# One diffusion-backbone layer on one core: 28 table slabs split and stored ahead of their stage, and one meeting of the engines where there were three

## The reference, cut to what matters

```python
# the merge behind the two mixers
(sigmoid(ga) * (attn @ w_up_a) + sigmoid(gb) * (ret @ w_up_b)) @ w_o
# PEER, in blocks of 128 tokens
s1, s2 = scores of the two query halves against 128 keys each, for 8 heads
16 best of each side, 16 best of their sums -> e (128 experts a token), g = softmax
a = gelu(x @ u_tab[e]);   out = (g * a) @ v_tab[e]
```

## Time and profile before

| | |
|---|---|
| Median of three runs | 2513.26 us |
| The profiled execution: its own time, its span | 2514.28 us, 2512.5 us |
| Busy share of the span | PE 91%, DVE 74%, ACT 48%, POOL 15% |
| Mean granted TensorE clock | 0.953 |
| Merge stage | 623.5 to 900 us |
| Table stage: LEAD, tiles, TAIL | 906 to 1097, 1097 to 1708.6, 1708.6 to 1801 us |
| Second table, residual, norm | 1809.5 us to the end |

### The profile page before, as it was taken

One profiled execution on the slowest core, in us unless ns is written; L12 is line 12 of the kernel. 1 busy time (PEld: TensorE's weight loads), 2 busy tenths in 40 slices (PEclk: granted clock), 3 DMA queues, 4 the chain that ended last, 5 costly groups with the idle time before them and its releaser, 6 DMA issues. The chain is left out here.

```text
span 2512.5 us, 34243 instructions
## 1 busy us (share of the span) xinstructions
PE 2290.0 (91%) x12048; PEld 1257.8 (50%) x12048; DVE 1857.6 (74%) x4157; ACT 1202.7 (48%) x1694; POOL 371.0 (15%) x267
## 2 busy tenths in 40 slices
PE   6799997985898979889899898999799999999997
PEld 3477664442665754435545455465344444444443
DVE  2555416455655357889989999885689999999999
ACT  1433433235444225555455454565645555555553
POOL 0000000000000000122222122232122222222220
PEclk9899998997998989999999899999899999999999
DMA  9421221000522144564676766889788778777881
GB/s 385 188 77 59 96 76 45 17 17 18 217 71 89 59 185 160 190 222 165 248 249 225 255 212 239 295 292 391 258 327 299 294 296 298 293 295 296 304 301 67
DMA packets 163392, 506.98 MB, mean 202 GB/s; under 512 B 14368, under 2 KB 47936, under 8 KB 155584
## 3 DMA queue, kind: packets, MB, share of 16 engines
q1 hardware_dynamic: 95440, 296.13, 33.0%
q0 software_dynamic: 36864, 134.23, 14.7%
q10 hardware_dynamic: 30960, 75.07, 7.8%
HBM read 421.93 MB, written 83.44 MB: 201 GB/s over the span
## 5 line engine op out<-in xcount | busy, mean ns | idle before, releaser
L210 ACT ACTIVATE lin_hi<-lin_raw,lin_wsc 128x1024 f16<-128x1024 f32 x196 | 224.3, 1146 | 414.5 <-DVE lin_wsc L123 326.3
L1747 POOL DMA_INDIRECT row<-u_rows_dram,picked x128 | 185.3, 1448 | 1505.8 <-DVE picked L2022 929.3
L231 PE MATMUL u_ps<-h_hi,lin_hi 128*128 128x512 f16 x1024 | 398.8, 389 | 7.5 <-PEq L64 7.5
L231 PE MATMUL u_ps<-h_lo,lin_hi 128*128 128x512 f16 x1024 | 397.6, 388 | 0.0
L231 PE MATMUL u_ps<-h_hi,lin_lo 128*128 128x512 f16 x1024 | 397.1, 388 | 0.0
L216 DVE SCALAR_TENSOR_TENSOR lin_lo<-lin_raw,lin_wsc,lin_hi 128x1024 f16<-128x1024 f32 x196 | 250.9, 1282 | 179.0 <-ACT lin_hi L210 178.9
L1683 POOL DMA_INDIRECT row<-v_dram,picked x128 | 178.4, 1394 | 490.8 <-DVE acc L2259 449.6
L175 ACT ACTIVATE lin_junk<-lin_raw 128x1024 bf16<-128x1024 f32 x196 | 204.5, 1043 | 62.9 <-DMA lin_raw<-w_all_dram 62.6
L2370 PE MATMUL y_ps<-region 128*128 128x512 f16 x512 | 194.9, 381 | 8.3 <-PEq L64 8.3
L2372 PE MATMUL y_ps<-region 128*128 128x512 f16 x512 | 194.8, 380 | 0.0
L2371 PE MATMUL y_ps<-region 128*128 128x512 f16 x512 | 194.8, 380 | 0.0
(11 more groups left out here) (378 smaller groups left out, 4124.1 us busy)
## 6 DMA issues: line engine op xcount, KB each, us to landing
lin_raw<-w_all_dram SPq DMA_DIRECT2D x196, 512.0 KB
act_scratch<-activated ACTq DMA_DIRECT2D x128, 256.0 KB
wgt_scratch<-region ACTq DMA_DIRECT2D x64, 512.0 KB
region<-v_dram SPq DMA_DIRECT2D x15, 2048.0 KB
oh_buf<-v_dram SPq DMA_DIRECT2D x15, 2048.0 KB
proj<-w_mod_dram SPq DMA_DIRECT2D x16, 1536.0 KB, 11.9
region<-wgt_scratch SPq DMA_DIRECT2D x16, 1024.0 KB, 9.7
region<-act_scratch SPq DMA_DIRECT2D x16, 1024.0 KB
```

What stands on the lines that cost most here:

```text
L210: nc.scalar.activation(self.hi[b][:], self.raw[b][:], ACT.Copy, scale=self.wsc[:, b:b + 1]).then_inc(self.sem("head", b), 1)
L231: last = nc.tensor.matmul(self.ps[b % 2][:, half, 0:ts.stop - ts.start], w_[:, kc, :], x_[:, kc, ts], start=(j == 0 and kc == 0), stop=(j ...
L1747: nc.gpsimd.indirect_dma_start(out=row[j % NG][:], out_offset=None, in_=a["u_rows"], in_offset=bass.IndirectOffsetOnAxis(ap=rows0[:, j:j + ...
```

## The change

Three things are done.

1. **28 slabs are split early.** They are those with b = 2 and 3 of the first 14 quads of the token tiles (quads `QA` to `QE` - 1: tiles 0 and 1 and the first 16 slabs of tile 2). Their loads, squares, heads and rests are made beside merge slabs 1 to 28, their scales four wide in the same instructions as those of the merge maps, and GpSimd's queue stores both halves (256 KB each) to a scratch array in device memory. In the tiles SP loads the two halves (2 x 256 KB) straight into `hi` and `lo`, where it loaded the raw slab (512 KB); ACT and DVE do nothing for these slabs but the gelu. The powers of two are kept in a small tile.
2. **`clear` becomes `retire` at three changes** (projection to attention, attention to merge, first to second table): only the block's own end is a meeting; GpSimd clears the dead semaphores inside the next block. The change from merge to first table keeps all three meetings.
3. **The last batch of a tile** is multiplied and evicted behind the next tile's first slab, and the tile loops of PE and SP are written out (they were hardware loops).

Core of the diff:

```diff
+            def load_pre(self, sp, q, b):
+                sp.wait_ge(self.sem("product", b), q)
+                for n, half in enumerate((self.hi[b], self.lo[b])):
+                    sp.dma_start(half[:, :, :].rearrange("p k m -> p (k m)"), pre_d[2 * (q - QA) + b - 2, n]
+                                 ).then_inc(s(f"pre_ld{b}"), 16)
...
             def product(self, pe, q, b, staged=None):
-                pe.wait_ge(self.sem("split", b), q + 1)
+                if self.pre(q, b):
+                    pe.wait_ge(s(f"pre_ld{b}"), 32 * (q - QA) + 32)
+                else:
+                    pe.wait_ge(self.sem("split", b), self.turn(q, b) + 1)
...
+                to = (q + (b + n) // 4, (b + n) % 4)
+                return to if b + n < 4 * left + 4 and not self.pre(*to) else None
...
                 @block.sync   # merge stage
+                    def load_pre_raw(sl):
+                        if (p := pre_slab(sl)) is not None:
+                            if p >= 4:
+                                sp.wait_ge(s("pre_split"), p - 3)
+                            sp.dma_start(pre_raw[p % 4][:], a["w_all"][4 * (QA + p // 2) + 2 + p % 2]).then_inc(...)
...
+                @block.gpsimd
+                def _(pool):
+                    for p in range(NPRE):
+                        pool.wait_ge(s("pre_split"), p + 1)
+                        for n, half in enumerate((pre_hi, pre_lo)):
+                            pool.dma_start(pre_d[p, n], half[p % 2][:]).then_inc(s(f"pre_st{p % 2}"), 16)
...
                 @block.scalar   # merge stage
+                    def pre_square(sl): ...          # waits for the load; ACT Square, as L175
+                    def pre_head(sl):
+                        if (p := pre_slab(sl)) is not None:
+                            act.wait_ge(lin.sem("scaled", p % 4 // 2), Q_UP + 2 + p // 4)
+                            if p >= 2:
+                                act.wait_ge(s(f"pre_st{p % 2}"), 32 * (p // 2))
+                            nc.scalar.activation(pre_hi[p % 2][:], pre_raw[p % 4][:], ACT.Copy, scale=...)
...
                         lin.act_slab(act, q, b, left)
+                        pre_head(sl + 3)
+                        pre_square(sl + 5)
...
                 @block.vector   # merge stage
+                    def pre_rest(sl): ...            # waits for pre_head; as L216, and a copy of one column
...
                         lin.dve_before(dve, q, b, left, inverse=sl + 1 not in (WO, WQ, LAST))
                         lin.dve_after(dve, q, b, left)
+                        pre_rest(sl + 3)             # ahead of the slab's eviction
...
                 def tile(t):    # table stage, PE
                     for m in range(PLAIN):
                         lin.pe_slab(pe, *at(t, m))
+                        if t and m == 0:
+                            gates(t - 1, NBATCH - 1)
...
-                    gates(t, NBATCH - 1)
-                run(pe, 0, NTD, tile)
+                for t in range(NTD):
+                    tile(t)
...
-        s.clear("vp_")
+        s.retire("vp_")
```

More of the change, by code:

```diff
@@ L153, in sem, with pre, turn, col @@
                 return s(f"{self.tag}_{what}{b}")
+            @staticmethod
+            def pre(q, b):
+                return b >= 2 and isinstance(q, int) and QA <= q < QE
+            @staticmethod
+            def turn(q, b):
+                if b < 2 or not isinstance(q, int) or q <= QA:
+                    return q
+                return QA if q < QE else q - (QE - QA)
+            @staticmethod
+            def col(b):
+                return slice(4 * (b // 2) + b % 2, 4 * (b // 2) + b % 2 + 1)
+            @staticmethod
+            def pre_col(p):
+                return slice(4 * (p % 4 // 2) + 2 + p % 2, 4 * (p % 4 // 2) + 3 + p % 2)
+            @staticmethod
+            def width(q):
+                return 4 if isinstance(q, int) and Q_UP < q < Q_U else 2
             @staticmethod
@@ new lines, in square @@
+            def square(self, act, q, b):
+                n = self.turn(q, b)
+                act.wait_ge(self.sem("loaded", b), 16 * n + 16)
+                act.wait_ge(self.sem("total", b // 2), n)
+                act.wait_ge(self.sem("square", (b + 3) % 4), n + 1 if b else self.turn(q, 3))
+                if b == 0 and self.pre(q - 1 if isinstance(q, int) else q, 3):
+                    act.wait_ge(self.sem("square", 1), q)
+                if b == 2:
+                    act.wait_ge(self.sem("square", 1), q + 1)
+                nc.scalar.activation(self.junk[:], self.raw[b][:], ACT.Square, accum_out=self.ssq[:, self.col(b)]
@@ L176, in square @@
                                      ).then_inc(self.sem("square", b), 1)
             def total(self, pe, q, g):
[L179 to L182, removed]
+                n, w = self.turn(q, 2 * g), self.width(q)
+                pe.wait_ge(self.sem("square", 2 * g), n + 1)
@@ L183, in total @@
+                pe.wait_ge(self.sem("square", 2 * g + 1), n + 1)
+                pe.wait_ge(self.sem("scaled", 1 - g), q + 1 if g else self.turn(q, 2))
+                if g == 0 and isinstance(q, int) and self.pre(q - 1, 2):
+                    pe.wait_ge(self.sem("scaled", 0), q)
+                if w == 4:
+                    pe.wait_ge(s("pre_sq"), 4 * (q - Q_UP - 1) + 2 * g + 2)
+                nc.tensor.matmul(self.total_ps[g][:, 0:w], ones[:], self.ssq[:, 4 * g:4 * g + w],
                                  start=True, stop=True).then_inc(self.sem("total", g), 1)
@@ L250, in wait_out, with ahead @@
                 eng.wait_ge(self.sem("product", b), q + 1)
-                eng.wait_ge(self.sem("inverse", b), self.inverses(q + 1))
+                if not self.pre(q, b):
+                    eng.wait_ge(self.sem("inverse", b), self.inverses(self.turn(q, b) + 1))
             def out(self, b):
                 return self.ps[b % 2][:, 0:2, 0:NH2]
-            @staticmethod
-            def ahead(q, b, n, left):
-                return (q + (b + n) // 4, (b + n) % 4) if b + n < 4 * left + 4 else None
+            def ahead(self, q, b, n, left):
+                to = (q + (b + n) // 4, (b + n) % 4)
+                return to if b + n < 4 * left + 4 and not self.pre(*to) else None
             def act_slab(self, act, q, b, left=2):
@@ L1688, in build @@
             NBATCH = P // OB
-            PLAIN, LEAD = 4, 32
             PIECES = 8
```

139 lines of the change are left out of this document (99 added, 40 removed).

## The result

The kernel after takes 2472.12 us (median, 2465.45 to 2473.3), beside 2513.94 us for the kernel before on the same chip: a ratio of 0.9828 (95% interval 0.9814 to 0.9842), 42 us less where 32 were forecast. The prediction of 2481 us was 9 us too high; the range 2467 to 2500 holds the result.

What follows compares the result with a forecast made beforehand. DVE was taken to bound the tiles, with PE nearly equal after the change, and PE the merge stage. Tiles -40, merge +15.2 and meetings -7.4 gave -32.2 us, so 2481 us against the 2513.26 median; range 2467 to 2500.

Steps and rivals of the forecast that it cites:

- a sum of 45.6 us: Tiles: DVE work and waits removed for 28 slabs, 12.2 + 16.7 + 16.7 us; 40 us taken as the gain.
- The last batch: Tile ends: PE's wait of up to 5.4 us goes, but its gain is inside the 40 us, not beside it.
- The merge stage, +15.2: Merge stage: added early-split work costs 15.2 us in sum, between 8 below and 30 above.
- UP, 8.1 us a slab and 9 in all: UP: early head and rest delay evictions, 8.1 us a slab where PE needs 6.6; 9 us over slabs 2 to 7.
- Start, 2.7: Merge start: the pair's total also needs two early slabs, 1 MB more in the load queue; 2.7 us.
- WO, 3.5 in a late eviction: WO: early head and rest make the eviction 0.7 us late, 0.3 at even b; 3.5 us over slabs 9 to 15.
- WQ and the stores, 0: WQ: added work hidden below PE's 6.6 us a slab; stores, estimated at 10 us at most, hidden too; 0.
- Meetings, -7.4: Three stage changes: second and third meetings dropped, with all of SP's waits there paid back; 7.4 us less.
- Clock in UP: Rival: merge stage pays twice as much, PE's clock falling in UP with its stops; 2494 us, chance 0.15.
- Half the gain: Rival: tiles gain only 25 us, PE and DVE holding each other up or halves arriving late; 2496 us, chance 0.12.
- The stores: Rival: in the merge stage the early head waits for the store of two slabs before; 2539 us at 16 us, chance 0.05.
- Hidden better, 2467: Rival: merge costs only 8 us and the tiles gain DVE's full 45.6 us; 2467 us, chance 0.08.

Runs made afterwards that it cites:

- run 4: Changed kernel with its merge-side work kept, but the tiles load and split every slab themselves as before: 2519.6 us, ratio 1.0016.
- run 5: Changed kernel with idle work on DVE in place of the 28 early slabs' rests and scales, 40 us in all: 2513.58 us, ratio 0.9991.
- run 7: Changed kernel with only 14 idle rests put back on DVE, 16.7 us: 2485.49 us, ratio 0.9872.
- run 6: Changed kernel with idle work on ACT, 28 copies and 28 squares, 61 us in all: 2470.27 us, ratio 0.9819.
- run 2: Kernel before with only the last batch moved behind the next tile's first slab and PE's and SP's tile loops written out: 2512.94 us, ratio 0.9995.
- run 3: Changed kernel with each tile's last batch back at the tile's end: 2474.55 us, ratio 0.9831.
- run 8: Changed kernel without the token tiles' 56 loads of halves and PE's wait for them, output part left out: 2472.45 us, ratio 0.9826.
- the seven and the three traces named above: Seven traces with the changed kernel's merge code, merge stage 295.3 to 299.6 us; three with the merge code before, 281.6 to 282.7 us.
- Run 11: As run 10, with loads of slabs 4 and 5 and the first two early slabs ahead of the gates' loads: 2463.67 us, ratio 0.9784.
- run 10: As run 9, with 32 slabs split early instead of 28: 2462.02 us, ratio 0.9789.
- run 9: Changed kernel with the early rest behind the slab's evictions in UP and WO instead of ahead of them: 2469.44 us, ratio 0.9819.
- Run 12: As Run 11, with early rest behind the next slab's scales, early square ahead of early head, x and keys loaded later: 2460.69 us, ratio 0.9781.
- run 1: Kernel before with one meeting instead of three at the three stage changes, nothing else: 2507.61 us, ratio 0.9971.

## Why the prediction was right, and where it was not

**The tiles.** The forecast took 40 us from a sum of 45.6 (14 rests, 10 pairs with their scales and a rest, 4 places of 3.05 us), because "PE and DVE are nearly equal, each waits for the other at times". Measured: 44.8 us from tile 0 to tile 3's picks, and 47 by the ratio of run 4, with its 5 us either way. Another 1.6 us are gone from the last six slabs of LEAD, but not by DVE's relief: in run 5, with DVE's work put back, these six still take 32.8 us (34.5 before, 32.9 in the changed kernel). Slab 30 of LEAD takes 6.1 us before, 5.2 after and 6.4 in run 4, where the early slabs are squared and totalled in the tiles again; the forecast had counted nothing for those totals. **The step that failed is the loss of 5.6 us put on that sum.** PE's busy time was taken as given, 448.8 of 449.9, but 16.4 us of it went with the waits: 432.3 us at a granted clock of 0.99, from 448.8 at 0.95. The slow stretches stood behind PE's waits for a late DVE, and were no floor beside it. The 433.5 worked out from tile 3's batches agrees with these 432.3; the stretch, at 450.5, is not down to it. Runs 5 and 7 show DVE setting the length on both sides, run 6 that what ACT loses counts for nothing. The forecast's signs for tiles 0 and 1, 143 and 140 us, came out as 139.3 and 138.9; DVE's share stayed over 90% (0.94).

**The last batch: nothing beside the 40.** Right, by runs 2 and 3. "DVE's picks are late next" is the smaller part of what takes its place: 2.0 us in run 2, against 7.7 at the totals.

**Loads of halves and SP's queue: 0.** Right, by run 8 and by the waits.

**The merge stage, +15.2.** It paid 13.0 between the two traces, and 14.1 by the medians of the seven and the three traces named above (296.3 and 282.2 us). The sum is right within what the stage varies; its parts are not all right.
- *UP, 8.1 us a slab and 9 in all.* 7.88 a slab; slabs 2 to 7 took 7.5 us more than before. The loop is the one described; its instructions overlap by a tenth of a microsecond here and there, which the forecast's sum did not have.
- *Start, 2.7.* 4.8: slabs 0 and 1 took 22.5 us, 17.7 before. The wait itself is 2.8 longer, as forecast (PE's total waits for the early square, 5.6 us in the row above). The other 2.0 are the products of the two slabs, which take 8.53 and 8.07 us where they took 7.95 and 6.68: the clock behind the waits, which the term had left out. Run 11 takes 5.3 off these two slabs, against run 10, by the order of the loads alone.
- *WO, 3.5 in a late eviction.* 1.8 over slabs 8 to 14, and PE stands **at another wait**: at a total that needs the early square on ACT, 1.2 us over three slabs:

```profile
PE mrg_spare L238 <- ACT pre_junk L1609: 1.2, 3, 0.5
```

  It stands ahead of the products on PE's queue. The forecast followed head, rest and eviction, and left out that the scales of the early slabs share a total with those of the merge maps, so that ACT's fifth instruction gates PE. The late eviction is part of it all the same, for ACT's slab begins behind it: with the early rest behind the eviction, in runs 9 and 10, slabs 12 and 14 took 7.0 us for 7.4. Run 12, which moved the square ahead of the early head, and the rest too, brought slabs 8 to 14 to 47.5, where they took 48.0 before the change.
- *WQ and the stores, 0.* WQ took 107.3 us beside 107.9; the stores landed in 2.3 to 7.6 us, and ACT never waited for one.
- About 1.2 us the other way lie in the norms, WQ's products and the scores together, the parts that vary by themselves.

**Meetings, -7.4.** PE's three waits fell by 2.3, 2.5 and 3.0, in all 7.8; run 1 gives 7.3.

**The rivals.** *Clock in UP:* the granted clock of UP is 0.90 where it was 0.95, but nearly all of that is in slabs 0 and 1, behind waits of 15.0 and 5.6 us (0.76 there, 0.92 before):

```profile
617.10:639.60 22.50, 16.83 (x98) 11.06 (x99) 8.45 (x17) 10.62 (x17) 1.31 (x2) 0.76 0.96 372
639.60:679.40 39.80, 34.49 (x248) 23.98 (x245) 27.46 (x47) 24.93 (x40) 4.94 (x10) 1.00 0.88 331
```

In slabs 2 to 6 PE stands still 0.8 to 1.2 us in every 7.9, and each burst runs at 2.4 GHz. The Trainium skill, "TensorE: Matmul & The Clock Gate", section "HAM oscillation — how this bites in real kernels", describes a kernel in which every burst of products starts cold behind a wait for a load. The waits of that kernel are longer than the stops here, so the trace does not speak against it. *Half the gain:* no, by run 4. *The stores:* not in the changed kernel; their landing was estimated at 10 us at most, and the real 7.6 fits. Run 12 shows the mechanism at work, with a store that took 12.5 us. The Trainium skill's rule on DVE and GpSimd's descriptors ("SBUF — State Buffer", section "🔬 SBUF: two separate sides") left no mark that this trace shows: in WQ DVE was at work 61.8 of 107.3 us, and all 56 stores of the stage landed within 7.6. Whether DVE's instructions there are of the kind that the rule names, no run here shows. *Hidden better, 2467:* the tiles' half of it came near (44.8 of 45.6), the merge stage's did not.

So the number was 9 us high. Between the traces the miss is 10.2 (42.4 against 32.2): 4.8 for the tiles, 2.2 for the merge stage, 0.4 for the meetings, 3.1 for LEAD and 1.7 for the start, with 2.0 of the other sign behind tile 3's picks. The 4.8 are the failed step; the 2.2 and the 1.7 are no larger than these parts vary from trace to trace.

## What to carry to other kernels

Where one engine set the stretch, what it lost came back nearly one for one (44.8 of 45.6 us), though a second engine looked nearly as long: part of that engine's busy time was slow clock behind the very waits that went. A busy share of 0.94 can be a full engine; the way to find out is to put idle work back and see whether the time follows. Work moved beside another stage is paid by the place that it takes in each queue: ask of every moved instruction what is due behind it, a total and a scale as much as an eviction, and of every moved load whose landing it delays.

## What was not expected of the hardware

- The granted clock over the tiles rose from 0.95 to 0.99 with waits of PE for picks and evictions that fell from 40 to 14 us, and PE's busy time fell by 16.4 us for nearly the same products.
- Stops of 0.8 to 1.2 us in every 7.9 left the clock at 1.00.
- A 256 KB store on GpSimd's queue landed in 2.3 to 7.6 us while the DMA engines were busy 0.5 to 0.9 of the time; in run 12 one took 12.5 us, beside loads of 2560 and 1024 KB.
- The part ahead of the merge stage, the same code each time, ended between 613.5 and 622.9 us, and the same merge stage took 295.3 to 299.6: more than most effects tried here, which single slabs and the steady stretch of the tiles show and whole times do not.
